# Head norms and routing places moved to GpSimd, gates kept in the slot table, and small joints reordered, in a two-layer transformer kernel with a mixture of experts

## What is computed

```python
def rms_norm(x, g):
    return x * rsqrt(mean(x * x, -1) + RMS_EPS) * g

# attention of the first block: 16 heads of 64; k and q are normed head by head
k = rms_norm(k.reshape(B, S, 16, 64), k_norm_g)
q = rms_norm(q.reshape(B, S, 16, 64), q_norm_g)
logits = q @ k.T * 64 ** -0.5 + cum_log_f[query] - cum_log_f[key]
o = softmax(causal(logits)) @ v
h = h + (o * sigmoid(gate)) @ w_out

# mixture of experts: x is rms_norm(h, m_norm_g), 256 rows
top_v, top_i = top_k(x @ w_router, 2)
top_w = softmax(top_v)
gates = sum(one_hot(top_i, 8) * top_w[..., None], axis=1)
for e in range(8):
    y = y + gates[:, e:e + 1] * ((silu(x @ a[e]) * (x @ b[e])) @ w_out[e])

# second block, last product of its mixer
mixed = concat([att, hm * sigmoid(mo)])
x = x + rms_norm(mixed @ w_out, g_mix_post)
```

## Time and profile before

| | |
|---|---|
| median of 3 runs | 1881.97 us |
| lowest, highest | 1876.48, 1882.63 us |
| the profiled execution | 1881.93 us, of which the span of the trace is 1880.3 us |
| TensorE busy | 98% of the span, 8848 matmuls |
| VectorE, ScalarE, GpSimd busy | 75%, 65%, 5% |
| mean granted TensorE clock | 0.994 of full speed |

### The profile page before, as it was taken

The page is one execution under the profiler, slowest core; times in us unless marked ns, Lnnn a source line. Parts: engine busy times, 40 slices in busy tenths (PEclk is TensorE's granted clock), DMA queues, the critical chain, the costliest instruction groups (busy, mean ns, idle before and its releaser), DMA issues.

```text
span 1880.3 us, 25646 instructions
## 1 busy us (share of the span) xinstructions
PE 1851.1 (98%) x8848; PEld 1553.1 (83%) x8848; DVE 1413.5 (75%) x1600; ACT 1214.1 (65%) x1353; POOL 102.1 (5%) x104
## 2 busy tenths in 40 slices
PE   9999999999899999999999999999999999999998
PEld 8998888888787888888888888888888788888887
DVE  6666476557667888888888888888888996587643
ACT  6544465447665777777677777777778675666542
POOL 2000000000002100000000000100001501000000
PEclk9999999999999999999999999999999998999999
DMA  9656566554239999999999999999999963445550
GB/s 290 190 173 224 180 186 194 180 179 159 95 134 318 335 394 395 394 394 393 394 395 394 378 386 373 382 379 372 387 373 371 387 259 101 135 135 168 179 191 34
DMA packets 237862, 516.16 MB, mean 275 GB/s; under 512 B 15260, under 2 KB 55312, under 8 KB 237792
## 3 DMA queue, kind: packets, MB, share of 16 engines
q1 hardware_dynamic: 232304, 499.70, 74.4%
q0 software_dynamic: 5184, 14.50, 2.1%
q10 hardware_dynamic: 304, 1.05, 0.2%
HBM read 506.78 MB, written 8.41 MB: 274 GB/s over the span
## 4 chain that ended last, share of the span: by engine, by line
PE 90%; DVE 5%; ACT 3%; issue 2%; DVEq 0%; ACTq 0%; POOL 0%; POOLq 0%
PE G L1466 23%; PE G L1468 22%; PE G L1467 22%; PE SM L1466 5%; PE SM L1468 5%; PE SM L1467 5%; PE T L1426 3%; DVE e_low L711 3%; ACT e_high L703 1%; PE T L1869 1%; PE SM L1654 1%; DVE dense_low L494 1%; ACT dense_high L474 1%; PE SM L1711 0%; PE SM L2013 0%
## 5 line engine op out<-in xcount | busy, mean ns | idle before, releaser
L711 DVE TENSOR_TENSOR e_low<-e_arrived,e_high 128x2048 fp32r<-128x2048 f32 (+1 forms) x346 | 765.2, 2265 | 78.0 <-ACT e_high L703 75.9
L703 ACT CAST e_high<-e_arrived 128x2048 fp32r<-128x2048 f32 x338 | 624.5, 1913 | 6.3 <-PE SM L1468 6.3
L1466 PE MATMUL G<-e_high,work_r 128*128 128x512 f32 x896 | 354.2, 395 | 6.7 <-DVE e_low L711 6.4
L1468 PE MATMUL G<-e_high,work_r 128*128 128x512 f32 x896 | 349.4, 390 | 0.0
L1467 PE MATMUL G<-e_low,work_r 128*128 128x512 f32 x896 | 348.8, 389 | 0.0
L1466 PE MATMUL G<-dense_high,xT_hi_all 128*128 128x512 f32 (+1 forms) x760 | 296.1, 390 | 1.7 <-ACT work_all L1062 0.7
L1468 PE MATMUL G<-dense_high,xT_lo_all 128*128 128x512 f32 (+1 forms) x760 | 284.7, 375 | 0.0
L1467 PE MATMUL G<-dense_low,xT_hi_all 128*128 128x512 f32 (+1 forms) x760 | 284.1, 374 | 0.0
L485 DVE TENSOR_TENSOR dense_low<-dense_raw,dense_high 128x2048 fp32r<-128x2048 f32 (+1 forms) x74 | 150.2, 2059 | 89.1 <-ACT dense_high L467 88.1
L1466 PEld LDWEIGHTS G<-e_high,work_r 128*128 128x128 f32 x896 | 168.2, 188 | 43.6 <-DVE e_low L711 9.9
L1468 PEld LDWEIGHTS G<-e_high,work_r 128*128 128x128 f32 x896 | 168.2, 188 | 36.0
(11 more groups left out here) (367 smaller groups left out, 2053.5 us busy)
## 6 DMA issues: line engine op xcount, KB each, us to landing
e_arrived<-in_m_w_in_dram SPq DMA_DIRECT2D x448, 512.0 KB
e_arrived<-in_m_w_out_dram SPq DMA_DIRECT2D x224, 512.0 KB
dense_raw<-in_a_w_in_dram SPq DMA_DIRECT2D x32, 768.0 KB, 6.4
dense_raw<-in_f_w_in_dram SPq DMA_DIRECT2D x44, 512.0 KB, 4.6
dense_raw<-in_w_up_dram SPq DMA_DIRECT2D x16, 1024.0 KB, 5.2
dense_raw<-in_w_down_dram SPq DMA_DIRECT2D x16, 1024.0 KB, 4.9
dense_raw<-in_a_w_out_dram SPq DMA_DIRECT2D x12, 1024.0 KB, 5.1
dense_raw<-in_f_w_out_dram SPq DMA_DIRECT2D x11, 1024.0 KB, 4.9
```

The costliest lines, as they stand in the source:

```text
L703: nc.scalar.copy(e_hi_unit(n), e_raw(n, e_arrived)).then_inc(e_hi, 1)
L711: ins = nc.vector.tensor_tensor(e_raw(n, e_low)[:, at], e_raw(n, e_arrived)[:, at], e_hi_unit(n)[:, at].bitcast(F32), ALU.subtract)
L1466: nc.tensor.matmul(bank, x_hi, w_hi, start=start, stop=False)
L1468: return nc.tensor.matmul(bank, x_lo, w_hi, start=False, stop=stop)
```

## The change

1. **Head norms** leave VectorE and ScalarE. For each (p, c) GpSimd does six small instructions on 128x8 (a power of -1/2 in place of root and reciprocal) and one product on 128x512. The transposes and copies of heads stand in other chunks for p = 2, and wait for `heads_scaled`.
2. **Joint to bo**: the first two `gated_turns2` stand after chunk (7, 3, 0) and not after the last one. ScalarE does `gated_high(0)` and `(1)` before the last `qk_copy`.
3. **Routing places** go to GpSimd (22 small instructions, reductions as chains of adds), which waits only for the gates.
4. **Gates** become a third column of the slot table. `dest_of` of the next turn is fetched with its gate at the end of a turn, and ScalarE multiplies by it where it copied before (`y_copy`). The multiplication at line 959 is gone. The additions to h come in halves, each after a given unit of the last turn has been split.
5. **Loop of the experts**: a Silu of one column stands at its head on ScalarE, and values are loaded into registers earlier.
6. **po**: the low part of its last unit is made by GpSimd, and VectorE waits for it before the first unit of `mu`.

```diff
+HEAD_TURNS = {0: {(3, 1): (0, 1), (3, 3): (2, 3)}, 1: {(2, 3): (0, 1), (3, 1): (2, 3)},
+              2: {(2, 2): (0,), (3, 0): (1,), (3, 2): (2, 3)}, 3: {(2, 3): (0, 1), (3, 1): (2, 3)}}
+HEAD_COPIES = {0: {(3, 2): ((0,), (1,))}, 1: {(3, 0): ((0,), (1,)), (3, 2): ((2,), (3,))},
+               2: {(2, 3): ((0,), ()), (3, 1): ((), (1,)), (3, 3): ((2,), (3,))}, 3: {(3, 0): ((0,), (1,)), (3, 2): ((2,), (3,))}}
...
-        homes = sb("homes", [P, 2, NT, 2], U32)
+        homes = sb("homes", [P, 2, NT, 3], U32)
...
+            def head_norms(p, c):
...
+                pool.wait_ge(head_summed, 2 * p + c + 1)
+                steps.then(nc.gpsimd.tensor_scalar(var, sums, 1.0 / HD, EPS, ALU.mult, ALU.add))
+                steps.then(nc.gpsimd.tensor_tensor(r, var, minus_half[:, mine], ALU.pow))
+                steps.then(nc.gpsimd.tensor_tensor(near, r, r, ALU.mult))
+                steps.then(nc.gpsimd.tensor_tensor(near, near, var, ALU.mult))
+                steps.then(nc.gpsimd.tensor_scalar(near, near, -0.5, 1.5, ALU.mult, ALU.add))
+                steps.then(nc.gpsimd.tensor_tensor(r, r, near, ALU.mult))
...
+                nc.gpsimd.tensor_tensor(x, x, r.rearrange("p (h e) -> p h e", e=1).to_broadcast([P, 8, HD]), ALU.mult).then_inc(heads_scaled, 1)
...
-            pool.wait_ge(places_ready, 1)
+            pool.wait_ge(gates_ready, 1)
...
+            steps.then(Q.tensor_tensor(first_rank, rank, best, ALU.mult))
+            by_expert(pick_rank[:, 0:NT], first_rank)
+            by_expert(pick_rank[:, NT:2 * NT], rank)
...
+            steps.then(Q.tensor_copy(homes[:, :, :, 2].bitcast(F32), picks(both)))
...
+                pool.dma_start(dest_of[:, :], slot_table[bass.ds(it * P + P, P), 1:3], allow_slow_non_contiguous=True
+                               ).then_inc(dest_landed, 16)
...
-                steps.then(nc.gpsimd.tensor_scalar(xn[:, 1, :], picked, both[:, NT * i + c:NT * i + c + 1], None, ALU.mult))
-                nc.gpsimd.tensor_tensor(h[:, c, :], h[:, c, :], xn[:, 1, :], ALU.add).then_inc(picked_added, 1)
+                for b in range(2):
+                    pool.wait_ge(e_lo, final * UNITS + (9 + 4 * (2 * n + b)))
...
+                    nc.gpsimd.tensor_tensor(h[:, c, at], h[:, c, at], picked[:, at], ALU.add).then_inc(picked_added, 1)
...
+            nc.gpsimd.tensor_tensor(unit_place(po_last, dense_low), unit_place(po_last, dense_raw), high_place(po_last).bitcast(F32),
+                                    ALU.subtract).then_inc(dense_lo, 1)
...
-                        if (q, kk) == (0, 0) and s - 1 in HEAD_SLABS:
-                            take_root(2 * 8)
...
-                nc.scalar.copy(y_rows[:, b * BANK:(b + 1) * BANK], SM[b][:, :]).then_inc(y_copied, 1)
+                act.wait_ge(dest_landed, it * 16 + 16)
+                nc.scalar.mul(y_rows[:, b * BANK:(b + 1) * BANK], SM[b][:, :], slot_gate).then_inc(y_copied, 1)
...
+                nc.scalar.activation(rinv[:, 0:1], rinv[:, 0:1], ACT.Silu)
...
+                        if (s, q, kk) == (7, 3, 0):
+                            for j in range(2):
+                                gated_turns2(j)
...
-                                head_variance(p)
...
-                                head_norms(p)
...
-            make_low(dve, unit_ahead2(pr.slabs, 1))
             mixed_low_half(1)
+            dve.wait_ge(dense_lo, split_count(po.first + po.units - 1))
             make_low(dve, mu.first)
```

More of the change, by code:

```diff
@@ L331, in build @@
         root = stats[:, 304:368]
+        head_variances, head_near = variance[:, 32:48], variance[:, 48:64]
+        head_root, minus_half = root[:, 32:48], root[:, 48:64]
         correction = stats[:, 184:216]
@@ L903, in _ @@
                            ).then_inc(zeros_landed, 16)
+            pool.dma_start(dest_of[:, :], empty_slots[:, 0, 1:3], allow_slow_non_contiguous=True).then_inc(dest_landed, 16)
             pool.wait_ge(xn_ready, 4)
@@ L1198, in _ @@
                             step(u)
-            qk_copy(qk.slabs - 1, 1)
             base = qk_base + len(TURN_NO)
@@ L1208, in _ @@
                 gated_high(j)
+            qk_copy(qk.slabs - 1, 1)
             for n in range(LEAD):
@@ L1231, in _, with gather_copy @@
             ins.then_inc(gap_exp, 1)
-            def gather_copy(it):
-                for half in range(2):
+            def gather_copy(it, halves=(0, 1)):
+                for half in halves:
                     act.wait_ge(gather_full, it * 2 + (half + 1))
@@ L1269, in _ @@
                         nc.scalar.activation(e_silu, G[2 * (s % 2)][:, :], ACT.Silu).then_inc(e_silu_ready, 1)
-            last = act.value_load(rounds_i[0:1, 1:2], min_val=E - 1, max_val=2 * E - 1)
             for b in range(2):
@@ L1794, in _ @@
                         forget_sums()
-                    if s == 7 and q == 3:
-                        for j in range(2):
-                            gated_turns2(j)
             base = qk_base + len(TURN_NO)
```

159 lines of the change are left out of this document (79 added, 80 removed).

## The result

The changed kernel takes 1865.94 us (median of five runs, 1861.20 to 1866.80). The kernel before, with two more runs, has a median of 1877.80 us. The ratio is 0.9925, interval 0.9913 to 0.9937. A later comparison on chip 7 gave 0.9917 (0.9903 to 0.9932). It is faster, by 12 us between the medians and by 14 by the ratio, where I had forecast 7.6. The time lies inside the range of 1864.5 to 1878.5. The size of the gain does not fit the forecast.

The account below looks back on a forecast made before the run. TensorE, busy 98% of 1880.3 us, was taken as the bound, leaving only its idle time and low-clock stretches. Terms -7.9 - 0.5 - 1.4 - 2.3 + 0.2 - 2.8 + 7.1 = -7.6 took 1881.9 to 1874.3 us, range 1864.5 to 1878.5.

Parts of the forecast that it names:

- head norms: First block's attention, slabs 4 and 5: shorter stalls 3.0 + 1.8 us, clock 3.1 us; gain 7.9 us, ends 5 to 9.8.
- joint to `bo`: Joint to bo: 0.7 of the 1.20 us wait stay for ScalarE's last copy; gain 0.5 us, ends 0 and 1.2.
- first turn: First turn of the experts: VectorE starts at 594.0, the stall falls from 2.18 to about 0.8 us; gain 1.4 us.
- every turn: Eight expert turns: the second table load before the first Silu goes, and with it eight stalls of 0.29 us; gain 2.3 us.
- places on GpSimd: First turn: 22 small GpSimd instructions beside VectorE's subtractions delay them; loss 0.2 us, between 0 and 1.5.
- last turn: Last expert turn: multiplications gone, additions in halves; of 3.1 us of waits 0.3 left, gain 2.8 us.
- low part in `po`: Last unit of po: GpSimd's subtraction blocks VectorE's small instructions, TensorE stands 4.6 us, low clock follows; loss 7.1 us.
- The eight stalls of 0.29 us go: Expert turns: with the second table load off the list, TensorE's wait of 0.29 us in each turn vanishes; 2.3 us.
- The rival in which this stall only moves: Slab 4: TensorE still waits over 3.5 us, the clock falls, 6 us of gain are missing; 1880.5 us, chance 0.10.
- the small instructions in po do not wait: po: VectorE's small instructions pass beside GpSimd, term -0.9, time 1866.3 us; chance 0.27 together with the half way case.
- the forecast's own range: Whole kernel: 1870.5 to 1878.5 us, by the ends of the forecast's terms; the forecast's chance 0.55.
- Both rivals: Expert turns: chain of places starves the second turn, about 1915 us, 0.04; second table load comes back, 1876.6 us, 0.04.

Follow-up runs that it names:

- experiment 2: Changed kernel without the Silu of one column at the head of the expert loop; 1870.17 us.
- experiment 3: Changed kernel with the transposes and copies of heads of p = 2 (slab 4) back in their old chunks, norms still on GpSimd; 1865.30 us.
- experiment 9: Kernel before with one edit, the products for the gate logits of the second block one chunk later; 1876.39 us.
- experiment 11: Changed kernel with second-block gate logits one chunk later and po's low part shared, three quarters VectorE, last quarter GpSimd; 1855.52 us.
- experiment 6: Changed kernel with GpSimd's low part in po in four instructions of 128x512 in place of one of 128x2048; 1860.96 us.
- experiment 4: Kernel before with only the head norms edit: arithmetic on GpSimd, new chunks, wait for heads_scaled; 1868.33 us, ratio 0.9940.

## Why the prediction missed

Against the profiled span the forecast was 7.6 us, and the traces differ by 19.4. The 11.8 us between them, term by term:

| term | forecast | measured | what was off |
|---|---|---|---|
| head norms | -7.9 | -10.3 | no wait left where 1.9 us were kept; price of a wait; clock |
| joint to `bo` | -0.5 | -0.4 | |
| first turn | -1.4 | -1.5 | |
| every turn | -2.3 | -4.5 | price of a wait |
| places on GpSimd | +0.2 | 0.0, in the turns' row | |
| last turn | -2.8 | -4.2 | price of a wait; nothing left over |
| low part in `po` | +7.1 | +6.4 | stall 3.28 us, not 4.6 |
| slow stretch in `pr` | 0 | -4.8 | in the profiled run of before by chance |

**The price of a wait** is the step that failed most often. "The eight stalls of 0.29 us go" was priced with the idle column, and each was 0.56 us (experiment 2). It is a quarter of a microsecond at each of some seventeen waits: 2.2 us in the turns, 1.1 in the last turn, some 1.4 in slabs 4 and 5, of which 0.4 belong to a delay just ahead of the long stall that no row of the view of waits shows. The number was in the trace of before. One need only have taken the distance of two starts, with the wait and without.

**Head norms.** I played the lists forward and kept 1.3 us in slab 4 and 0.6 in slab 5. With both engines free of the norms TensorE waited 0.17 us. The new chunks were needed for that: with the old ones 1.90 us came back (experiment 3), so the argument from the bank T0 was right. The low clock had cost 2.1 to 2.4 us and not 3.1, and this too varies: in the profile of experiment 9, the same code up to here, the products behind the same stall of 4.30 us start 1.3 us earlier. GpSimd's power of -1/2 took 1.64 us where I had 0.9 at most for a small instruction, but a chain of seven took 5.0 to 6.5 us, within the 2 to 7 allowed. The rival in which this stall only moves has fallen.

**The low part in po** went as the forecast said, and this was the edit on which the forecast turned. The small instruction waited 4.21 us, `mixed_low_half(0)` came late, TensorE stood 3.28 us where I had 4.6, and the low clock came behind it. The sizes that were off: the subtraction took 4.56 us and not 5.1, and the low half began 0.33 us behind its end and not 1.0. The low clock was less severe in the second profile of the changed kernel (0.74 and 0.92 in the two windows), and the loss 1.3 us smaller, so it varies with the run. The rule of the Trainium skill, "SBUF — State Buffer", section "Who interferes with whom", is borne out for instructions of 4 elements by the 4.21 us. The 0.18 us of the reciprocal and the 1.13 us of experiment 11 agree with its other half, that VectorE with at most one input in SBUF is not held up. The 1.20 us of the TENSOR_SCALAR in experiment 6 is the case that the same section makes an exception of, since that operation can run in a mode that takes the shared pair.

The rival "the small instructions in po do not wait" had the time 1866.3, which is almost the measured 1865.9. Its mechanism is false all the same. The 8 us that it saved in `po` were gained elsewhere. Without the rows one would have taken it for confirmed. That the time lies in my range at all is luck of the same kind: the forecast's own range ended at 1870.5, and what lies below it was there for a free case that did not happen. Two numbers of the prediction also do not follow from its terms. Free small instructions make 8.0 us, from +7.1 to -0.9, and not 8.5, and the moved stall gives 1874.3 + 6 = 1880.3 and not 1880.5.

**The slow stretch in pr** was in no term. The step that failed was the base of the sum: I read the clock only behind the stall that I was pricing and took the profiled run for typical because it stood at the median of three. The three runs lay at 1876.5, 1882.0 and 1882.6, and the two groups were to be seen there. Against the median of five, 1877.80, the change gains 11.9 us, and group against group (1876.0 to 1878.2 and 1861.4 to 1863.1 on one chip) 15. Like against like the forecast was thus half of the gain, and what is missing, some 7 us, is the price of the waits (4.7) and the stalls that I kept and that did not come.

The chain of places ran from 588.23 to 609.67, 21 us where I had allowed 48, and no turn waited for its rows. Second table loads did not come back. Both rivals fell.

## What to carry to other kernels

Price a wait of TensorE from start to start against the same place undisturbed; the idle column leaves out what the record before it covers, here 0.25 us at each. In these runs work given to GpSimd was free only while VectorE had no instruction of two SBUF inputs, however small, in front of something that TensorE needs (the small TENSOR_SCALAR of experiment 6 waited as well); so look at what is queued on VectorE during those microseconds, cut the instruction, or release it beside work that reads PSUM. When few runs of a kernel lie in two groups, look for a stretch of low granted clock in the profile before any difference is explained.

## What the runs showed of the hardware

- The length of a wait alone does not decide whether TensorE's clock falls from 2.4 to 1.2 GHz behind it. Behind 1.90 us (experiment 3) and 2.09 us (experiment 4) it fell. Behind 2.18 us in the kernel before and 2.10 us at the same place in experiment 9 it stayed at 1.00. I had put the point near 3.5 us, between the 2.18 and the 4.30 of the rows.
- Two runs of the same code can differ in this. In slab 5 the kernel before and experiment 9 have the same instructions and waits of 0.6, 0.7 and 0.9 us, and behind the last of them the window from 500 to 505 us is at 1.00 in the first and at 0.67 in the second:

```profile
500.00:505.00 5.00, 3.99 (x22) 3.32 (x23) 4.25 (x15) 3.01 (x10) 0.00 (x0) 1.00 0.01 3
```

```profile
500.00:505.00 5.00, 4.73 (x18) 3.91 (x19) 4.09 (x12) 2.11 (x10) 0.00 (x0) 0.67 0.01 3
```

- A stretch in which TensorE is busy throughout can run at half clock. Behind matmuls of 8 columns and a wait of 0.5 us it fell to 0.50 in the profiles of the kernel before and of experiments 3 and 4, worth 4.8 us, and stayed at 1.00 in those of seven others. That one kernel has both is concluded from its times.
- VectorE's instructions with two SBUF inputs wait for GpSimd one instruction at a time: one piece of 4.56 us delayed one small instruction by 4.05, four pieces delayed three small ones (the third a TENSOR_SCALAR) by 0.8 to 1.0 each. A reciprocal (0.18 us) passed beside GpSimd.
- GpSimd's 22 small instructions beside VectorE's subtractions took 0.19 to 2.34 us each, depending on whether a subtraction was running.
